# Neighbourhood attention with values stationary and head pairs in PSUM halves, its last steps inside a row-by-row output projection

## The reference, cut to what matters

```python
q, k, v, u, vs = _project(h, w_in, q_gain, k_gain)     # 8 heads of 64
s_win = einsum(q, k window) * scale + bias              # 256 keys, masked by the bias
s_ctx = einsum(q, k_ctx) * scale                        # 256 context keys
p = softmax(concatenate([s_win, s_ctx]))
o_na = einsum(p, [v, v_ctx])                            # 256 x 512
o_sg = gelu(u) * (w_s @ layernorm(gelu(vs)) + b_s)      # 256 x 512
y = concatenate([rms(o_na), rms(o_sg)]) * out_gain
x = x + g_a * (y @ w_out)
hf = rms(x) * (1 + sc_f) + sh_f                         # then router and experts
```

## Time and profile before

| | us |
|---|---|
| median of 3 runs | 1542.69 |
| lowest, highest | 1541.89, 1543.91 |
| the profiled execution, its own time | 1542.04 |
| its span, from the first to the last instruction | 1540.2 |

### The profile page before, as it was taken

How to read it: one execution, slowest core, us unless ns; L and a number is a source line. 1 busy time by engine, 2 the same in 40 slices (tenths; PEclk the granted TensorE clock), 3 DMA queues, 4 the chain that set the end, 5 groups by cost and what they waited for, 6 DMA issues and landing times.

```text
span 1540.2 us, 20164 instructions
## 1 busy us (share of the span) xinstructions
PE 1512.9 (98%) x7920; PEld 1257.1 (82%) x7920; DVE 1186.7 (77%) x1639; ACT 948.8 (62%) x1503; POOL 80.1 (5%) x78
## 2 busy tenths in 40 slices
PE   9999999999999999999999999999999899999997
PEld 9998888888888799888788887887777778888785
DVE  7568857667888684788576679877667789999998
ACT  6577854755444364878457555544455568888884
POOL 0010000000000000100000000000200000000005
PEclk9999999999999999999999999999999999999999
DMA  7545436437776445453455368884521449999994
GB/s 293 209 142 205 149 137 218 148 127 277 254 269 242 161 177 187 159 191 136 164 191 192 137 244 326 333 321 142 192 103 55 159 188 366 367 380 372 374 365 163
DMA packets 52200, 339.33 MB, mean 220 GB/s; under 512 B 7835, under 2 KB 8477, under 8 KB 13316
## 3 DMA queue, kind: packets, MB, share of 16 engines
q1 hardware_dynamic: 48932, 331.79, 58.3%
q0 software_dynamic: 3168, 6.20, 1.1%
HBM read 332.82 MB, written 10.49 MB: 223 GB/s over the span
## 4 chain that ended last, share of the span: by engine, by line
PE 47%; DVE 6%; ACT 2%; issue 1%; DMA 0%; POOL 0%; DVEq 0%; ACTq 0%
PE bank L842 14%; PE bank L844 13%; PE bank L843 13%; PE bank L848 3%; DVE wls L2285 2%; PE bank L1380 1%; DVE h L2255 1%; ACT whs L1603 1%; PE bank L1362 1%; PE bank L1182 0%; PE bank L1160 0%; DMA raw<-in_ws_dram 0%; PE bank L1099 0%; POOL sm L3256 0%; PE bank L1122 0%
## 5 line engine op out<-in xcount | busy, mean ns | idle before, releaser
L2285 DVE TENSOR_TENSOR wls<-raw,whs 128x1024 fp32r<-128x1024 f32 x432 | 514.1, 1226 | 149.0 <-ACT whs L1603 148.1
L1603 ACT ACTIVATE whs<-raw 128x1024 fp32r<-128x1024 f32 x432 | 435.9, 1052 | 189.1 <-PE bank L844 164.2
L842 PE MATMUL bank<-whs,P1h 128*128 128x512 f32 (+1 forms) x732 | 291.3, 398 | 2.0 <-issue 2.0
L844 PE MATMUL bank<-whs,P1l 128*128 128x512 f32 (+1 forms) x732 | 285.0, 389 | 0.0
L843 PE MATMUL bank<-wls,P1h 128*128 128x512 f32 (+1 forms) x732 | 284.1, 388 | 0.0
L842 PE MATMUL bank<-whs,P0h 128*128 128x512 f32 (+1 forms) x632 | 251.6, 398 | 1.4 <-DVE P0l L2255 1.4
L844 PE MATMUL bank<-whs,P0l 128*128 128x512 f32 (+1 forms) x632 | 245.1, 388 | 0.0
L843 PE MATMUL bank<-wls,P0h 128*128 128x512 f32 (+1 forms) x632 | 244.5, 387 | 0.0
L842 PEld LDWEIGHTS bank<-whs,P1h 128*128 128x128 f32 x732 | 138.0, 188 | 29.9 <-issue 3.4
L844 PEld LDWEIGHTS bank<-whs,P1l 128*128 128x128 f32 x732 | 137.9, 188 | 29.6
L843 PEld LDWEIGHTS bank<-wls,P1h 128*128 128x128 f32 x732 | 138.2, 189 | 26.7
(11 more groups left out here) (298 smaller groups left out, 2521.9 us busy)
## 6 DMA issues: line engine op xcount, KB each, us to landing
raw<-in_ws_dram SPq DMA_DIRECT2D x264, 1024.0 KB, 4.8
landing<-in_ws_dram SPq DMA_DIRECT2D x38, 1024.0 KB, 7.2
lnb<-in_ln_g_dram SPq DMA_DIRECT2D x6, 512.0 KB, 6.1
lnb<-in_ln_b_dram SPq DMA_DIRECT2D x6, 512.0 KB, 7.2
ydram<-arena POOLq DMA_DIRECT2D x4, 512.0 KB, 8.4
mid<-in_bias_dram SPq DMA_DIRECT2D x1, 2048.0 KB, 7.5
h<-in_x_dram SPq DMA_DIRECT2D x2, 512.0 KB, 4.0
lnb<-in_mem_dram SPq DMA_DIRECT2D x1, 1024.0 KB, 12.4
```

What stands on the lines that cost most here:

```text
L842: e.matmul(out, x[0], w[0], start=start, stop=False, skip_group_check=skip)
L844: return e.matmul(out, x[1], w[0], start=False, stop=stop, skip_group_check=skip)
L1603: e.activation(hi, src, ACT.Copy, bias=0.0, scale=1.0).then_inc(*high.done(n, f))
L2285: e.tensor_tensor(lo, src, f32(hi), ALU.subtract).then_inc(*low.done(n, f))
```

## The change

The scale -1/8 goes into q where it is written. DVE subtracts the bias in PSUM (window columns only) and takes the minimum there; ACT takes the exponential from PSUM with scale -1. DVE takes the reciprocal of the sums per pair, and ACT scales the probability rows in place before they are transposed. The copies of the transposes are shared, even heads on ACT, odd heads on DVE. A pair's values are stationary, 64 columns each, and write the two halves of bank 6, features on rows: the result is already in columns. ACT squares it and PE sums the squares over features with matmuls of one moving column; ACT and DVE apply the gain and split it from bank 6 into `na_cols`. The root-mean-square factor of na is applied in `merged2`; the sg rows are multiplied by its inverse.

There are 17 steps. 14, 15 and 16 run at the ticks of the output projection (now `fine=True`), whose order is all of row tile 0, then row tile 1. The work that closed the attention stands in `joined`, at the end of pair 1. The feeds inside the projection keep their places.

The plan of steps and the buffers:

```diff
-        ona = flat(memT[:, 0:4, :]).rearrange("p (t d) -> p t d", t=2)
+        squared = [flat(memT[:, 2 * t:2 * t + 2, :]) for t in range(2)]
...
+        PT2 = [*(arr(2048 + 512 * i, 4, 128) for i in range(3)), quarters(squared[1])]
...
+        na_cols = [[quarters(flat(cT[0][:, :, :])[:, 1024 * p + 512 * t:1024 * p + 512 * t + 512]) for p in range(2)]
+                   for t in range(2)]
...
+        STEPS2 = 17
         PAIR_AT = {**{i: i for i in range(0, 14, 2)}, 13: 14}
-        BY_VEC = (13, 14, 15)
+        SCALE_AT = {**{s + 1: s for s in range(0, 14, 2)}, 14: 14}
+        TURN_AT = {**{s + 2: (s,) for s in range(0, 12, 2)}, **{s + 3: (s + 1,) for s in range(0, 12, 2)},
+                   14: (12, 13), 15: (14, 15)}
+        WEIGH_AT = {5: 0, **{s + 4: s for s in range(2, 12, 2)}, 15: 12, 16: 14}
+        TURN_BANK = {13: 5, 15: 5}
         FEED_AT = (0, 1, 2, 5, 7, 8, 9, 11, 12)
-        MIX_SEQ = ((0, 0), (1, 0), (0, 1), (1, 1), (2, 0), (3, 0), (2, 1), (3, 1))
+        MIX_SEQ = ((0, 0), (1, 0), (2, 0), (3, 0), (0, 1), (1, 1), (2, 1), (3, 1))
```

PE:

```diff
-                    bank(4 + o, (vec, "sc2", i + o))
+                    bank(4 + o, (act, "ex2", i + o))
...
+                b = TURN_BANK.get(i, 7)
+                pe.wait_ge(act, "pn2", i)
+                bank(b, ((act, vec)[i % 2], "pT2", i))
...
+                pe.wait_ge(act, "pT2", i)
+                pe.wait_ge(vec, "pT2", i + 1)
...
                 for j in range(4):
-                    m = e.matmul(banks[6][:, hd * 64:(hd + 1) * 64], PT2[i % 3][:, j, :], vt[:, j, hd * 64:(hd + 1) * 64],
-                                 start=j == 0, stop=j == 3)
+                    for o in range(2):
+                        m = e.matmul(banks[6][64 * o:64 * o + 64, 64 * hd:64 * hd + 128],
+                                     vt[:, j, (hd + o) * 64:(hd + o + 1) * 64], PT2[(i + o) % 4][:, j, :],
+                                     start=j == 0, stop=j == 3)
                 m.then_inc(*mm.done("w2", i))
+            def square_sums(t):
+                pe.wait_ge(act, "nasq", t)
+                bank(4, (vec, "reps", "na", t))
+                for k in range(4):
+                    m = e.matmul(banks[4][:, 0:1], squared[t][:, k * 128:(k + 1) * 128], allone[:, 0:1], start=k == 0, stop=k == 3)
+                m.then_inc(*mm.done("nass", t))
...
+                      13: [(cond_rows, 0)], 14: [(square_sums, 0)]}
 
             def attention2():
-                n = len(items)
-                for i in range(n + 5):
-                    if i >= 5:
-                        weigh2(i - 5)
-                    if 3 <= i < n + 3:
-                        turn2(i - 3)
+                for i in range(STEPS2):
+                    for x in TURN_AT.get(i, ()):
+                        turn2(x)
                     if i in PAIR_AT:
                         scores2(PAIR_AT[i])
                     for f, *at in beside.get(i, ()):
                         f(*at)
+                    if i in WEIGH_AT:
+                        weigh2(WEIGH_AT[i])
...
+            def joined():
+                W.finish_side()
+                mm.here("merge")
+                W.raw_unit += [None] * 2
+                W.load()
+                issued["cst"] = W.dma
+                W.feed(1)
+            def y2_of(k, t):
+                return part_of(na_cols[t], slice(None), k) if k < 4 else part_of(PA, slice(None), k, slice(t * 128, (t + 1) * 128))
...
+                at={(1, 1): lambda: y_columns(0, 7), (1, 4): joined, (2, 2): lambda: square_sums(1), (2, 4): lambda: W.feed(1),
+                    (3, 4): lambda: W.feed(2), (4, 1): lambda: y_columns(1, 5), (4, 4): lambda: W.feed(1),
+                    (5, 4): lambda: W.feed(1), (7, 1): lambda: f_columns(0, True)}, fine=True)
```

ACT:

```diff
+            def exps(i):
+                for x in (i, i + 1):
+                    ac.wait_ge(vec, "nm2", x)
+                    if x >= 4:
+                        ac.wait_ge(mm, "pT2", x - 4)
+                    wait_for(ph2)
+                    put(S2[x % 4], banks[4 + x % 2][:, :], ACT.Exp, "ex2", x, bias=nm2[:, x:x + 1], scale=-1.0,
+                        acc=dn2[:, x:x + 1])
+            def weights(i):
+                ac.wait_ge(vec, "rd2", i)
+                for x in (i, i + 1):
+                    put(S2[x % 4], S2[x % 4], ACT.Identity, "pn2", x, scale=dn2[:, x:x + 1])
...
+                put(PT2[i % 4], ps4(TURN_BANK.get(i, 7)), ACT.Copy, "pT2", i)
...
+            def na_squares(t):
+                ac.wait_ge(mm, "w2", 8 * t + 6)
+                put(squared[t], banks[6][:, :], ACT.Square, "nasq", t)
+            def na_high(t):
+                na_squares(t)
+                for k in range(4):
+                    put(na_cols[t][0][:, k, :], ps4(6)[:, k, :], ACT.Identity, "fm", "y2", t, 0, 0, scale=ogain[:, k:k + 1])
...
+            beside = {2: [(gelu_v,)], 11: [(na_high, 0)], 14: [(gate_u, 0)], 15: [(gate_out, 0)], 16: [(gate_u, 1)]}
...
+                    if i in SCALE_AT:
+                        weights(SCALE_AT[i])
+                    for x in TURN_AT.get(i, ()):
+                        turn2(x)
                     if i in FEED_AT:
                         W.feed(1)
-                    if i < n:
-                        scores2(i)
+                    if i in PAIR_AT:
+                        exps(PAIR_AT[i])
...
+            def joined():
+                W.finish_side()
+                na_high(1)
+                act.here("merge")
+                gate_out(1)
+                W.raw_unit += [None] * 2
+                W.load()
+                W.feed(1)
```

DVE (and POOL's mark "merge" now stands before its four powers):

```diff
-                    ts(dst[:, :, kcol[j]:kcol[j] + 128], ps4(6 + j % 2), gain, None, ALU.mult, None, "qk", j)
+                    ts(dst[:, :, kcol[j]:kcol[j] + 128], ps4(6 + j % 2), gain, 1.0 if j < 4 else -0.125, ALU.mult, ALU.mult, "qk", j)
...
+                for x in (i, i + 1):
+                    t, hd = items[x]
+                    s_ = banks[4 + x % 2][:, 0:256]
+                    ve.wait_ge(mm, "sc2", x)
+                    ve.wait_ge(landed["bias"])
+                    tt(s_, s_, bias[:, t, hd, :], ALU.subtract, "sc2", x)
+                for x in (i, i + 1):
+                    ve.wait_ge(vec, "sc2", x)
+                    wait_for(ph2)
+                    red(nm2[:, x:x + 1], banks[4 + x % 2][:, :], ALU.min, "nm2", x)
...
+            def weights(i):
+                ve.wait_ge(act, "ex2", i + 1)
+                recip(dn2[:, i:i + 2], dn2[:, i:i + 2], "rd2", i)
+            def turn2(i):
+                if i % 2:
+                    ve.wait_ge(mm, "pT2", i)
+                    if i >= 4:
+                        ve.wait_ge(mm, "w2", i - 5)
+                    wait_for(ph2)
+                    copy(PT2[i % 4], ps4(TURN_BANK.get(i, 7)), "pT2", i)
...
+            def na_low(t):
+                ve.wait_ge(act, "fm", "y2", t, 0, 0)
+                for k in range(4):
+                    stt(na_cols[t][1][:, k, :], ps4(6)[:, k, :], ogain[:, k:k + 1], f32(na_cols[t][0][:, k, :]),
+                        ALU.mult, ALU.subtract, "fm", "y2", t, 0, 0)
+                vec.here("na", t)
...
+                i, x = 5 + 2 * t, vb[:, t, :]
+                ve.wait_ge(pool, "rpow", "na", t)
+                ve.wait_ge(pool, "rpow", "sg", t)
+                tt(evens[:, t:t + 1], ss[:, i - 1:i], rs_[:, i - 1:i], ALU.mult, "before")
...
+                ts(x, x, rs_[:, i:i + 1], evens[:, t:t + 1], ALU.mult, ALU.mult, "rms", "sg", t)
...
+                      9: [(gate_add, 1)], 10: [(cond_rows, 1)], 11: [(na_low, 0), (cond_rows, 2)], 12: [(cond_rows, 3)], 13: [(cond_rows, 0)],
+                      15: [(na_eps, 0), (gate_out, 0)]}
...
+            def joined():
+                W.finish_side()
+                gate_out(1)
+                na_low(1)
+                vec.here("merge")
+                sg_eps(1)
+                W.raw_unit += [None] * 2
+                W.load()
+                W.feed(1)
...
-                tt(o, banks[2 * c + t][:, :], gab[:, 0, s_], ALU.mult, "mo", t, c)
+                ve.wait_ge(pool, "rpow", "na", t)
+                stt(o, banks[2 * c + t][:, :], rs_[:, 4 + 2 * t:5 + 2 * t], gab[:, 0, s_], ALU.mult, ALU.mult, "mo", t, c)
...
+                (0, 4): lambda: (sg_eps(0), sg_rows(0)), (1, 1): lambda: y_columns(0, 7), (1, 4): joined, (2, 4): lambda: (W.feed(1), na_eps(1)), (3, 2): lambda: sg_rows(1),
+                (3, 4): lambda: W.feed(2), (4, 1): lambda: y_columns(1, 5), (4, 4): lambda: W.feed(1),
+                (5, 4): lambda: W.feed(1), (7, 1): lambda: f_lows.extend(f_columns(0, True))}, fine=True)
```

More of the change, by code:

```diff
@@ L655, in build @@
         S2 = [arr(512 * i, 512) for i in range(4)]
-        PT2 = [arr(2048 + 512 * i, 4, 128) for i in range(3)]
+        PT2 = [*(arr(2048 + 512 * i, 4, 128) for i in range(3)), quarters(squared[1])]
         mx2, nm2, dn2 = smv(256, 16), smv(272, 16), smv(288, 16)
@@ new lines, in na_low, with na_eps @@
+            def na_low(t):
```

(47 more changed lines are left out.)

108 lines of the change are left out of this document (21 added, 87 removed).

## The result

The changed kernel takes 1547.3 us (median of 8 runs, 1545.96 to 1549.09) against 1541.89 for the kernel before on the same chip: ratio 1.0031, 95% interval 1.0020 to 1.0042. It is slower, by some 5.4 us. The span of its profiled execution is 1545.5 us.

The account below looks back on a forecast made before the run. PE was taken to bound attention and projection. Terms of +2.8 us up to the last scores and +4.4 after gave +7.2 on 1542.04, 1549.2, put at 1550 by the median; range 1539 to 1555, likeliest 1546 to 1553 (0.50).

Parts of the forecast that it names:

- The end moves one for one: Experts behind the attention neither shorten nor stretch, so what the attention gains or loses moves the end equally.
- Weighing: PE in attention: eight pairs at 1.2 us, 9.6, in place of 16 heads at 0.84, 13.4; 3.8 us less.
- Other PE work: Two sets of na transposes go (-0.9 us); two sums of squares come at 0.85 each (+1.7).
- rival D: PE's work falls by 3 us only; a shrinking tail without the end moving is part of the forecast; no separate chance.
- Waits of steps 0 to 10: Attention, small PE waits: 0.5 us at transpose 2, 0.4 at the first weighing, 0.3 at transpose 8.
- Steps 11 to 13: From r, DVE's reciprocal for pair 10: PE waits 1.65 us weighing heads 8, 9 and 1.75 before pair 14's scores.
- Bank 0: Entry into the projection: DVE empties the bank at r + 15.1, PE comes at r + 12.3; wait 2.75 us.
- Inside the projection: Waits 0.5 and 1.3 us around sg transposes, 2.65 and 3.4 for weights of units 2 and 3, 0.75 before (2,1).
- Rival C: Slower: column halves don't overlap (+3, 1553), or half clock (about 1.6 us per eight matmuls), or longer waits (1555); chance 0.12.
- Rival B: No PE wait for units 2 and 3, or no softmax waits: about 6 us go, 1543.7; with half-sized waits, chance 0.21.
- Rival A: Faster queues: six ACT-DVE chains each 1.2 us shorter make the change even, 2 us shorter -4.5 (1538); chance 0.17.
- The signs: For: PE idle 3 us before fourth pair, 2 to 3 inside third, DVE pause 4; against: no such idle, span under 94.

Follow-up runs that it names:

- e4: Changed kernel with the two heads of a pair weighed one after the other in place of in turn: 1552.45 us, ratio 1.0072.
- e1: Changed kernel with weight halves of units 2 and 3 split earlier, at attention steps 13 and 14 and the end of pair 1: 1540.36 us, ratio 0.9996.
- e2: Changed kernel with the condition row that occupies bank 0 made at step 9 in place of step 13: 1547.57 us, ratio 1.0036.
- e3: Changed kernel; in step 11 ACT's high halves precede its weight half and DVE's row addition its low halves: 1548.78 us, ratio 1.0039.
- e8: Changed kernel with e3's edit plus 7 matmuls of no use in the wait for bank 0: 1545.76 us, ratio 1.0023.
- e7: Changed kernel with the edits of e1, e2 and e3 together: 1540.12 us, ratio 0.9989 to the kernel before.
- e9: e7 with transposes 13 and 15 in bank 1 in place of bank 5: 1536.75 us, ratio 0.9974 to the kernel before.
- e10: e7 with 8 matmuls of no use in the wait before transpose 13: 1537.79 us, ratio 0.9981 to the kernel before.
- e5: Changed kernel with 14 matmuls of no use in PE's wait before pair (3,0): 1545.82 us, ratio 1.0031.
- e12: Changed kernel with matmuls of no use in four waits (7, 5, 7 and 14), no wait shortened: 1545.45 us, ratio 1.0035.

## Why the prediction came out as it did, step by step

*The end moves one for one.* Held: +5.9 in the stretch, +5.4 in the time.

*Weighing.* 1.2 us a pair was taken, 1.02 measured, 1.13 with the 0.11 that the matmul behind it loses (its next start is 0.34 us later in place of 0.23). The row of the first block's halves was the right neighbour, and the weight loads, twice as many here, cost nothing more. 0.6 to 1.4 us of the sum was mis-sized here. e4 shows that alternating is what makes it cheap.

*Other PE work.* Held: 0.88 and 0.81 for the two sums of squares (taken 0.85). PE's busy time fell by 1.2, or some 2.8 without the 1.6 of low clock, where rival D said 3.

*Waits of steps 0 to 10.* 0, 0.25 and 0.22 for 0.5, 0.4 and 0.3.

*Steps 11 to 13.* The mechanism held: a DVE pause of 3.86 (about 4 was said), waits of 1.05 and 1.45 for 1.65 and 1.75. The sizes were off by PE, which reached the weighing at r + 4.15 (taken r + 3.7), and by DVE, where two minima from PSUM take 1.2 us from start to start, where I had added two of 0.69.

*Bank 0.* 1.78 for 2.75: the same quicker DVE, r + 13.6 for r + 15.1.

*Inside the projection.* 0.22, 1.30, 1.89, 3.42, 0.80 for 0.5, 1.3, 2.65, 3.4, 0.75. The 3.42 hangs on four DVE instructions behind pair (2,0) and came out exactly; the 1.89 was 0.75 shorter since ACT began the high half 1.1 us behind the head of the pair, where I had counted 1.8, and since PE came there 0.2 later.

*The clock.* Rival C had it as a possibility behind long waits; it came once, 1.6 us, outside my sum. Without it the sum would have missed by 2.9 us and not by 1.3. The sum had 3.6 us too much waiting (15.95 for 12.38), saved 0.7 too much of PE's work and had no low clock: that these partly cancel, so that the total is nearer than its terms, is luck. The other half of rival C, halves that don't overlap, is refuted by the 1.02 and by e4. Rival B (the halves in time) is what e1 built: 6.5 us of the distance, the low clock's 1.6 among them, where I had said 6.

*The rivals' sums.* Rival A takes 2 us off each of six waits, but three of the six are shorter than 2 us; at most 10.7 us could go, which is 3.5 below the kernel before and not 4.5.

*The signs.* Those named for the forecast are there, with 1.89 a little under the 2 to 3 inside the third pair; none of those against it is.

## What to carry to other kernels

When a change brings work forward, look first at where each engine's feeding instructions stand in its queue: here three weight halves, behind instructions that wait for the very engine that needs them, cost 6.5 us with the low clock behind them, more than twice the 2.8 us of PE work that the change saved, and moving them brought it back. Don't judge a wait by taking it away alone: the next wait or a lower clock can take the gain (e2, e3, e8), and it did so with three edits together (e7), until one more wait (e9) or the clock (e10) was mended. Look for a free bank before reordering anything: the waits of 1.78 (bank 0) and of 2.01 in e7 (bank 5) were for a bank that still held something else.

## What the hardware showed that I had not expected

In the changed kernel TensorE's clock falls at 1201.1, as the wait of 3.42 us begins (1201.2) and not after it, and work in that wait alone doesn't keep it up (e5); with work in four waits it stays at 1.00 (e12). So the fall comes of PE's thin work before, and not of the wait beside which it shows. How much work, and where, is enough isn't shown. In the changed kernel a wait of 1.78 us left the clock at 1.00; in e3 the same 1.78, behind last scores that came 1.5 us earlier, is followed by 0.50, though the waits before it are shorter there (none and 0.85, in place of 1.05 and 1.45). Why stays open. The Trainium skill ("TensorE: Matmul & The Clock Gate", Part 1) says that the gate goes by how busy PE has been recently; e5 against e12 agrees, and e3 isn't explained by that alone.

Matmuls of no use kept the clock at 1.00 in e10, e12 and, up to 1197, e8. Where they fit into a wait at full clock they cost nothing (transpose 13 in e10 and pair (3,0) in e12 start where they did); in e5 they came when the clock had fallen, and cost 1.0 us.

Two column halves whose records alternate take 1.02 us for 16 records, one half after the other 1.51: a factor of 1.48. The Trainium skill ("TensorEngine Tiling (Array Packing)", Theoretical Speedup) gives up to two, which this doesn't reach.
